# One RWKV chain of 16 matrices in 32-row blocks in place of two chains of 8 in 64-row blocks

## The chip, the cores and the metric

The kernel runs on one core of a Trainium2 chip. The metric is device time in microseconds (us) from the start to the end of one execution.

## The reference, cut to what matters

A decoder trunk of two layers on 256 tokens of 1024 channels, all in fp32. Each layer has a SwiGLU FFN, a token mixer, and a second FFN. The mixer projects the tokens once and runs two branches (RWKV-7 with 8 heads of 64 channels, mLSTM with 4 heads of 128), each merged through a gate of its own:

```python
g_r, g_m = jnp.split(jax.nn.sigmoid(p_g.astype(jnp.float32)), 2, axis=-1)
return ((g_r * y_r + g_m * y_m) @ w_out).astype(h.dtype)
```

The RWKV branch is a recurrence over time, for every head:

```python
sa = jnp.einsum('bhvk,bhk->bhv', s, a_t)
s = s * w_t[:, :, None, :] + sa[..., None] * b_t[:, :, None, :] + v_t[..., None] * k_t[:, :, None, :]
y = jnp.einsum('bhvk,bhk->bhv', s, r_t)
```

The kernel cuts the 256 tokens into 4 chunks of 64. Inside a chunk the recurrence becomes products with 64x64 matrices; one of them is the inverse of (I - N), where N is strictly lower triangular. There are 8 heads x 4 chunks = 32 such matrices a layer.

## The kernel before

Everything is one program with a hand-written order for each engine, and semaphores between them. `mm` (L1792) issues each matmul, `turn` (L1796) each transpose on TensorE; `act` (L680) is every ScalarE operation. An fp32 matmul appears in the trace as two records of weight load and two of matmul, a transpose as one.

In the mixer of a layer TensorE runs, after the projections and the mLSTM products: gate products "num", the turned mLSTM heads, the RWKV chain, the low-rank product "g", gate products "tail", then `branch` m and r and the output product. A gate product is a 128x128 weight tile times 256 tokens, 8 of them accumulate to one tile; 96 of them (6 tiles of 2 x 8 products, `gates`, `GATE_PLACES`) are scattered as lumps over the RWKV chain, so that TensorE has work while VectorE and ScalarE bring one step's result from PSUM to SBUF for the next. There are 24 lumps of 2 to 14.

The chain goes over two groups g of 4 heads (2 pairs q, 2 tiles t of 128 tokens, 2 heads h of a pair), so 8 matrices with the two chunks c of a tile in the lower and upper 64 partitions: 16 matrices of 64x64 a group. In each group:

- "m_t", "m_n": products of a, r with b, k, masked on VectorE (L1625, L1630) into nt (N transposed), mrb, mak, mrk and the three parts n16, o32, o64 of N (blocks of 16; what 32 adds; what 64 adds). Heads and chunks here use all four quadrants of the array.
- v, a, b, k are turned (4 whole 128x128 transposes each).
- The inverse: powers of the 16-blocks p2, p4, p8 and the running product xt, then the steps to 32 and to 64. Each is a `batch` n of 4 matrices x 2 chunks, the chunk c from rows c to columns c of the array: two places. ScalarE copies a power (L680), VectorE adds to xt (`grow`, L1651) and transposes in blocks (`flipped`, L1646).
- "z0" (mak times v), "uz" (xt times a and z0), then "gt", "h", "qt", the local part of y (`y_local`), the chain over chunks (`chain`, L1692) and "y".

The order of the inverse on TensorE, with the gate lumps between:

```python
for n in range(2):
    batch("p4", n, 0, p2t, p2, [AC.at(l, f"p2 {g} {n}"), DV.at(l, f"p2t {g} {n}")])
    batch("xt 2", n, 2, p2, xt, [DV.at(l, f"xt 1 {g}"), DV.at(l, f"m_n {g} 2")])
gates(f"inverse {g} a")
for n in range(2):
    batch("p8", n, 0, p4t, n16, [AC.at(l, f"p4 {g} {n}"), DV.at(l, f"p4t {g} {n}")])
    batch("xt 4", n, 2, n16, xt, [DV.at(l, f"xt 2 {g} {n}")])
```

VectorE computes y_m of the mLSTM branch (L1611) just before "m_t"'s masks. The head statistics (`head_sums`, `head_scaled`) of group 0 lie inside the chain of group 1; those of group 1 come after its y, while TensorE does "g" and "tail"; `y_turned(0)` comes before branch m, `y_turned(1)` after half of it. Weights come through a ring in SBUF, loaded by SP in order; one slot holds RWKV operands of group 1 until "qt 1", and SP waits for that before it loads branch weights into it.

Of the kernel before, what the change touches and what calls it, by code (L numbers as in the profile page):

```python
# [28 lines left out]
ALU = mybir.AluOpType  # L29
# [3 lines left out]
P = 128  # L33
# [97 lines left out]
def pair_uses(label):  # L131
# [6 lines left out]
GATE_PLACES = (("num", 4), ("heads", 4), ("masks 0 a", 8), ("masks 0 b", 4), ("inverse 0 p", 2), ("inverse 0 a", 2), ("inverse 0 b", 2),  # L138
# [112 lines left out]
def trunk(nc, numbers, x_in, c_in, ada_w, ada_b, norm_g, ffn_w_in, ffn_w_out, mix_w_in, rwkv_mu, rwkv_w0,  # L251
          rwkv_w_up, rwkv_a0, rwkv_a_up, rwkv_g_up, rwkv_k_k, rwkv_k_a, rwkv_r_k, rwkv_ln_g, rwkv_ln_b,
          conv_w, conv_b, gate_b, mlstm_ln_g, branch_r, branch_m, w_out, final_g, out):
    with ExitStack() as ctx:  # L254
# [44 lines left out]
        mask_t = sb("mask_t", [P, 4, 64])  # L299
        mask_n = sb("mask_n", [P, 3, 64])  # L300
# [46 lines left out]
        v_tm = carve(2, TT, P)  # L347
        b_tm = carve(2, TT, P)
        k_tm = carve(2, TT, P)
        az = carve(8, P)  # L350
        region = taken[0]
        layer_sets = [[group_set(set_0), group_set(ring[:, 1024 * held:1024 * held + SLOT])] for held in HELD]
# [16 lines left out]
        taken[0] = region  # L369
        m_t = carve(8, 4, 64)  # L370
        m_n = carve(3, 8, 64)
        p2, p2t, p4t, xt = (carve(8, 64) for n in range(4))
        uz = carve(8, P)
        qt = carve(4, P)
        gt_s = carve(4, 64)
        s_s = carve(4, 64)
        h_s = carve(6, 64)
        diag = carve(4, 64)
# [135 lines left out]
        def _(sp):  # L514
# [36 lines left out]
            for l in range(DEPTH):  # L551
# [16 lines left out]
                for n in range(4):  # L568
# [3 lines left out]
                    if use == HELD_TO:  # L572
                        sp.wait_ge(*DV.at(l, "qt 1"))
# [20 lines left out]
        def _(po):  # L594
# [51 lines left out]

            full = y_r[:, 0, 0:P]
            for n, (size, first) in enumerate(((16, 1), (64, 0), (64, 1), (64, 0))):
                fill(full, 1.0)
                keep(full, ALU.is_ge, -first, [[1, P]], -1, 0.0)  # L650
                diagonal_blocks(full, size)
                of_chunks(mask_t[:, n, :])
            for n, size in enumerate((16, 32, 64)):
# [3 lines left out]
                of_chunks(mask_n[:, n, :])  # L657
            for n in (2, 1):
                po.wait_ge(*PO.last(None))
                po.tensor_tensor(mask_n[:, n, :], mask_n[:, n, :], mask_n[:, n - 1, :], ALU.subtract)\  # L660
# [1911 lines left out]
```

## Time and profile before

| | us |
|---|---|
| median of 3 runs (1440.42 to 1440.79) | 1440.57 |
| the profiled execution: its span (the time shown for it) | 1437.0 |
| TensorE matmuls busy | 1419.4 |
| VectorE busy | 1048.7 |
| ScalarE busy | 298.9 |
| from gates "num" to the end of "tail", each layer | 94.67 |

The span runs from the first to the last instruction of one profiled execution; the runs' times are of other executions and hold what lies around it. TensorE is busy in 99% of the span, so a time saved on another engine shows only where TensorE waits for it, and the length of a TensorE record holds its latency: rates are read from differences of starts.

### The profile page before, as it was taken

The page shows a single profiled execution, that of the slowest core. Times are in us where ns is not written, and L with a number is a line of the kernel's source. Part 1 is how long each engine was busy: PE and PEld are TensorE (multiplying, and loading weights), DVE is VectorE, ACT ScalarE, POOL GpSimd, SP SyncE. Part 2 cuts the span into 40 slices and gives each one's busy share as a digit, 9 for nine tenths or more (in the row PEclk, how much of TensorE's full clock was granted, in tenths as well). Part 3 has the DMA queues.
Part 4 walks back from the last instruction along what each step waited for, and adds up shares of the span by engine and source line. Part 5 has one row for each costly group of instructions (what it writes and reads, how often), then busy time and mean ns, then how long its engine had stood idle before and what let it go on. Part 6 is the DMA issues. An engine that isn't in the chain of part 4 may idle for free.

```text
span 1437.0 us, 29272 instructions
## 1 busy us (share of the span) xinstructions
PE 1419.4 (99%) x12848; PEld 1332.5 (93%) x12848; DVE 1048.7 (73%) x1792; ACT 298.9 (21%) x586; POOL 72.2 (5%) x142
## 2 busy tenths in 40 slices
PE   7999999999999999999999999999999999999998
PEld 3999999898988999999999999988898889999998
DVE  5899888787634669987988886787972456756656
ACT  3111102532223031110031110045222311211101
POOL 7100000000000000000000000000000000000000
PEclk9999999999999999999999999999999999999999
DMA  9998876243422657887758876364432247466440
GB/s 348 336 335 302 306 290 195 89 132 104 117 62 90 227 188 260 296 300 292 248 193 266 285 275 235 127 166 132 133 103 61 61 147 263 148 206 205 179 145 30
DMA packets 214046, 283.03 MB, mean 197 GB/s; under 512 B 13288, under 2 KB 177504, under 8 KB 213920
## 3 DMA queue, kind: packets, MB, share of 16 engines
q1 hardware_dynamic: 194976, 211.11, 45.0%
q0 software_dynamic: 17952, 69.21, 13.2%
q8 instruction: 101, 1.65, 0.5%
q10 hardware_dynamic: 992, 0.85, 0.2%
q14 instruction: 25, 0.20, 0.0%
HBM read 280.10 MB, written 1.05 MB: 196 GB/s over the span
## 4 chain that ended last, share of the span: by engine, by line
PE 97%; DMA 1%; SPq 1%; DVE 1%; issue 0%; ACT 0%; ACTq 0%; DVEq 0%
PE ps L1792 96%; DMA arena<-in_ada_w_dram 1%; PE ps L1796 1%; SPq L549 0%; SPq L544 0%; DVE arena L1651 0%; DVE hT L1777 0%; DVE arena L1646 0%; DVE x L1191 0%; ACT xn L680 0%; ACTq L254 0%; SPq L542 0%; SPq L541 0%; DVEq L1776 0%; ACTq L994 0%
## 5 line engine op out<-in xcount | busy, mean ns | idle before, releaser
L1792 PE MATMUL ps<-hT,ring 128*128 128x128 f32 (+2 forms) x2448 | 399.4, 319 | 1.3 <-ACT hT L680 1.3
L1792 PEld LDWEIGHTS ps<-hT,ring 128*128 128x128 f32 (+1 forms) x2448 | 348.1, 190 | 35.5 <-issue 8.6
L1792 PE MATMUL ps<-y_both,arena 128*128 128x128 f32 x2304 | 266.6, 275 | 1.0 <-issue 1.0
L1792 PEld LDWEIGHTS ps<-y_both,arena 128*128 128x128 f32 x2304 | 261.8, 192 | 1.5 <-issue 1.5
L1792 PEld LDWEIGHTS ps<-arena 64*64 64x64 f32 (+1 forms) x3792 | 221.4, 153 | 17.0 <-issue 11.2
L1792 PE MATMUL ps<-arena 64*64 64x64 f32 (+3 forms) x3792 | 235.4, 243 | 1.3
L1792 PE MATMUL ps<-arena,ring 128*128 128x128 f32 (+1 forms) x1312 | 186.5, 294 | 0.0
L1792 PEld LDWEIGHTS ps<-arena,ring 128*128 128x128 f32 x1312 | 171.3, 192 | 6.6
L1018 DVE SCALAR_TENSOR_TENSOR ada_acc<-ada_stage,cond,ada_acc 128x1024 f32<-128x1024 f32 (+1 forms) x119 | 149.0, 1252 | 5.8 <-DMA ada_stage<-in_ada_w_dram 2.2
L1792 PE MATMUL ps<-y_both,ring 128*128 128x128 f32 (+1 forms) x1024 | 150.8, 301 | 0.0
L1792 PEld LDWEIGHTS ps<-y_both,ring 128*128 128x128 f32 x1024 | 138.6, 192 | 6.4
L673 POOL DMA_DIRECT2D ada_stage<-in_ada_w_dram x64 | 45.9, 717 | 1223.5 <-DVE ada_acc L1018 637.6
L1792 PE MATMUL ps<-hT,arena 128*128 128x128 f32 x640 | 78.0, 275 | 0.0
L1792 PEld LDWEIGHTS ps<-hT,arena 128*128 128x128 f32 x640 | 74.7, 192 | 0.0
L1247 DVE TENSOR_TENSOR arena<-ring 128x512 f32<-128x512 f32 x44 | 30.4, 690 | 47.1 <-PE ps L1792 46.8
L680 ACT ACTIVATE xn<-ps 128x128 f32<-128x128 f32 (+2 forms) x18 | 6.9, 383 | 273.7 <-PE ps L1792 273.7
L1121 DVE TENSOR_TENSOR raw<-raw,ps 128x256 f32<-128x256 f32 x40 | 16.8, 420 | 59.1 <-ACT raw L744 58.8
L680 ACT ACTIVATE arena<-ps 128x256 f32<-128x256 f32 (+3 forms) x90 | 39.4, 461 | 80.8 <-PE ps L1792 76.8
L736 ACT ACTIVATE raw<-ps 128x256 f32<-128x256 f32 x40 | 15.4, 386 | 189.9 <-PE ps L1792 189.9
L1232 DVE TENSOR_TENSOR arena<-ring 128x1024 f32<-128x1024 f32 x40 | 48.8, 1219 | 5.5 <-DMA ring<-in_ffn_w_in_dram 5.5
L1238 DVE TENSOR_TENSOR arena<-ring,arena 128x1024 f32<-128x1024 f32 x40 | 49.0, 1225 | 1.4
L1236 DVE TENSOR_TENSOR arena<-arena,ring 128x1024 f32<-128x1024 f32 x40 | 48.7, 1218 | 0.0
(306 smaller groups left out, 1371.8 us busy)
## 6 DMA issues: line engine op xcount, KB each, us to landing
ring<-in_ffn_w_in_dram SPq DMA_DIRECT2D x86, 1024.0 KB, 7.8
ada_stage<-in_ada_w_dram POOLq DMA_DIRECT2D x66, 1024.0 KB, 5.9
ring<-in_ffn_w_out_dram SPq DMA_DIRECT2D x44, 1024.0 KB, 6.2
ring<-in_mix_w_in_dram SPq DMA_DIRECT2D x46, 512.0 KB, 5.0
ring<-in_mix_w_in_dram SPq DMA_DIRECT2D x12, 1024.0 KB, 5.7
ring<-in_mix_w_in_dram SPq DMA_DIRECT2D x6, 1536.0 KB, 6.2
ring<-in_mix_w_out_dram SPq DMA_DIRECT2D x8, 1024.0 KB, 5.2
arena<-in_ada_w_dram SPq DMA_DIRECT2D x6, 1024.0 KB, 13.7
```

The lines of the kernel that those rows point to most:

```text
L673: po.dma_start(wide_stage(v), unit_rows(layer, col, h)).then_inc(ada_full[v % 2], 16)
L680: nc.scalar.activation(out_, in_, func, **kw).then_inc(*AC.step(label))
L736: nc.scalar.activation(part[:, 0, :], ps[:, bank_x, 0:256], ACT.Copy).then_inc(x_copied, 1)
L1018: V.scalar_tensor_tensor(dst, stage[:, k, :], cond[:, k0 + k:k0 + k + 1], dst, ALU.mult, ALU.add).then_inc(ada_done, 1)
L1121: free(V.tensor_tensor(part[:, 0, :], part[:, 0, :], ps[:, bank_w, 0:256], ALU.add))
L1232: V.tensor_tensor(s1, a21, a22, ALU.add).then_inc(w_summed, 1)
L1236: V.tensor_tensor(s2, s1, a11, ALU.subtract).then_inc(w_summed, 1)
L1238: V.tensor_tensor(s4, a12, s2, ALU.subtract).then_inc(w_summed, 1)
L1247: V.tensor_tensor(s1, a21, a22, ALU.add).then_inc(w_summed, 1)
L1792: return nc.tensor.matmul(out_, lhsT, rhs, start=start, stop=stop, **kw)
L1796: return nc.tensor.transpose(out_, in_, ident[0:n, 0:n])
```

## The change

The two groups become one chain: a step takes 16 head-and-tile pairs, 32 matrices, instead of 8 and 16. Every chunk stays in its own half of the partitions (`home`).

- N is made once by 64 products "n" with 32 columns of weights (`quarter`): diagonal 32-blocks and the off-diagonal block. nt is no longer a product: VectorE transposes n16. "mrb" and "kr 0/1" (mak and mrk side by side in mk) are made later, between steps of the chain.
- The inverse works on 32x32 blocks, four of them on the diagonal of the array (`blocks`). `power` multiplies the transposed power pt with px, which holds the power and the running inverse side by side: one product of 64 columns gives the next power and the product to add. Steps: "p2", "px 4", "px 8", "x 8" (inverse of the 16-blocks), "g32", "x 32" (of the 32-blocks), "g64", "xo" (the off-diagonal 32-block), all put together in xf. PO clears its zero block.
- v, b, k are turned by halves of the rows (16 transposes of 64 rows each), a whole (8).
- "uz" to "y" as before, for all 16; ScalarE and VectorE share the copies of uz.
- One lump of gate products a stage: 14 lumps of 4 to 27.
- The statistics of all heads come after the last y; both `y_turned` come after half of branch m. SP waits for "qt".

The diff, cut:

```diff
-GATE_PLACES = (("num", 4), ("heads", 4), ("masks 0 a", 8), ("masks 0 b", 4), ("inverse 0 p", 2), ("inverse 0 a", 2), ("inverse 0 b", 2),
-               ("inverse 0 c", 2), ("uz 0", 2), ("y 0 a", 5), ("y 0 b", 4), ("y 0 c", 2), ("next", 3),
-               ("masks 1 a", 8), ("masks 1 b", 4), ("inverse 1 p", 2), ("inverse 1 a", 5), ("inverse 1 b", 2),
-               ("inverse 1 c", 4), ("uz 1", 2), ("y 1 a", 5), ("y 1 b", 4), ("y 1 c", 2), ("tail", 14))
+GATE_PLACES = (("num", 5), ("n", 6), ("a", 6), ("b", 6), ("c", 5), ("d", 6), ("e", 5), ("f", 6), ("g", 5), ("h", 5),
+               ("i", 4), ("j", 5), ("k", 5), ("tail", 27))
...
+        mrb = carve(16, 64)
+        o64 = carve(16, 32)
+        mk = carve(16, P)
+        xf = carve(16, 64)
...
+        px = carve(2, 16, 32)
+        pt, xt, o32 = (carve(16, 32) for n in range(3))
...
-                        sp.wait_ge(*DV.at(l, "qt 1"))
+                        sp.wait_ge(*DV.at(l, "qt"))
...
+                        po.wait_ge(*PE.at(l, "num"))
+                        po.memset(xf[32:64, :, 0:32], 0.0).then_inc(*PO.step())
+                        po.memset(xf[96:128, :, 0:32], 0.0).then_inc(*PO.step(f"xf {l}"))
...
+                def power(label):
+                    ac.wait_ge(*PE.at(l, label))
+                    for g in range(2):
+                        if g:
+                            ac.wait_ge(*DV.at(l, f"{label} 1"))
+                        act(px[:, 0, 8 * g:8 * g + 8], view(ps[:, 2 + g, :], 8, 64)[:, :, 0:32], ACT.Copy, f"{label} {g}")
...
+                def grow(label, tile):
+                    dv.wait_ge(*PE.at(l, label))
+                    free(V.tensor_tensor(flat(tile), flat(tile), ps[:, 2, :], ALU.add), label)
+
+                def power(label):
+                    dv.wait_ge(*PE.at(l, label))
+                    for g in (1, 0):
+                        part = px[:, 1, 8 * g:8 * g + 8]
+                        if not g:
+                            dv.wait_ge(*AC.at(l, f"{label} 0"))
+                        free(V.tensor_tensor(part, part, view(ps[:, 2 + g, :], 8, 64)[:, :, 32:64], ALU.add), f"{label} {g}")
+                    flipped(None, pt[:, 0:8], px[:, 0, 0:8])
+                    dv.wait_ge(*AC.at(l, f"{label} 1"))
+                    flipped(f"{label} turned", pt[:, 8:16], px[:, 0, 8:16])
...
+                dv.wait_ge(*PE.at(l, "n"))
+                masked(px[:, 0], "n16", 0)
+                dv.wait_ge(*DV.last(l))
+                flipped("nt16", pt, px[:, 0])
+                free(V.tensor_tensor(px[:, 1], px[:, 0], spread[:, :].unsqueeze(1).broadcast_to([P, 16, 32]), ALU.add),
+                     "x 1")
+                masked(o32, "o32", 1)
+                dv.wait_ge(*AC.at(l, "p2"))
+                flipped("p2t", pt, px[:, 0])
+                dv.wait_ge(*PE.at(l, "mrb"))
+                for h in range(2):
+                    free(V.tensor_tensor(mrb[:, h::2, :], view(ps[:, 4 + h, :], 8, 64),
+                                         mask_t[:, 0, :].unsqueeze(1).broadcast_to([P, 8, 64]), ALU.mult),
+                         "mrb" if h else None)
+                power("px 4")
+                power("px 8")
+                masked_mk(0)
+                grow("x 8", px[:, 1])
+                dv.wait_ge(*DV.last(l))
+                flipped("x16", xt, px[:, 1])
+                masked_mk(1)
+                grow("x 32", xt)
+                dv.wait_ge(*DV.last(l))
+                flipped("x64", pt, xt)
+                for r in range(4):
+                    rows, at = slice(32 * r, 32 * r + 32), 32 * (r % 2)
+                    free(V.tensor_copy(xf[rows, :, at:at + 32], xt[rows, :, :]))
+                dv.wait_ge(*PE.at(l, "xo"))
+                free(V.tensor_copy(xf[64:96, :, 32:64], view(ps[64:96, 2, :], 16, 32)), "xf")
...
-                    for n in range(2):
-                        dv.wait_ge(*AC.at(l, f"p2 {g} {n}"))
-                        flipped("p2t", n, p2t, p2)
-                    for n in range(2):
-                        dv.wait_ge(*AC.at(l, f"p4 {g} {n}"))
-                        flipped("p4t", n, p4t, m_n[:, 0])
-                        grow("xt 2", n)
-                    if g:
-                        head_sums(l, y_heads[0], 8, 64, head_sq, "r 0")
-                    for n in range(2):
-                        grow("xt 4", n)
-                    for size, label in ((32, "xt 8"), (64, "xt 32")):
-                        for n in range(2):
-                            grow(label, n)
-                            dv.wait_ge(*DV.last(l))
-                            flipped(f"x{size}", n, p2t, xt)
-                    for n in range(2):
-                        grow("xt 64", n)
...
+                def turned(name):
+                    source = {"v": lambda q, t: raw[:, 8 + q, 1 + t * P:1 + t * P + P],
+                              "b": lambda q, t: sets[q // 2][3][:, 0, q % 2, t * P:t * P + P],
+                              "k": lambda q, t: sets[q // 2][3][:, 1, q % 2, t * P:t * P + P]}[name]
+                    for q in range(4):
+                        for t in range(TT):
+                            at = 64 * (2 * q + t)
+                            for h, hh in enumerate(chunks):
+                                last = nc.tensor.transpose(ps[:, h, at:at + 64], source(q, t)[hh], ident[hh, hh])
+                    last.then_inc(*PE.step(f"turned {name}"))
...
+                def blocks(label, bank, lhsT, rhs):
+
+                    for i in range(16):
+                        for rows in quarter:
+                            last = mm(ps[rows, bank, 32 * i:32 * i + 32], lhsT[rows, i, :], rhs[rows, i, :])
+                    last.then_inc(*PE.step(label))
...
+                def power(label):
+
+                    for i in range(16):
+                        at = 64 * (i % 8)
+                        for rows in quarter:
+                            last = mm(ps[rows, 2 + i // 8, at:at + 64], pt[rows, i, :], px[rows, :, i, :])
+                    last.then_inc(*PE.step(label))
+
+                pe.wait_ge(*DV.at(l, "prep 1"))
+                turned_heads()
+                pe.wait_ge(*DV.at(l, "gates 0"))
+                for q, t, h, hh in heads:
+                    ar, bt, kt, hats = sets[q // 2]
+                    at = 64 * (2 * q + t)
+                    for r, rows in enumerate(quarter):
+                        begin = t * P + 64 * (r // 2)
+                        last = mm(ps[rows, h, at + 32 * (1 - r % 2):at + 64], ar[hh, q % 2, t, 0, rows],
+                                  bt[hh, q % 2, begin:begin + 32 + 32 * (r % 2)])
+                last.then_inc(*PE.step("n"))
+                gates("n")
...
+                pe.wait_ge(*DV.at(l, "nt16"))
+                pe.wait_ge(*DV.at(l, "gates 1"))
+                blocks("p2", 2, pt, px[:, 0])
...
+                last.then_inc(*PE.step("mrb"))
+                gates("a")
+                pe.wait_ge(*DV.at(l, "p2t"))
+                power("px 4")
+                pe.wait_ge(*AC.at(l, "o64"))
+                turned("v")
+                gates("b")
+                pe.wait_ge(*DV.at(l, "px 4 turned"))
+                power("px 8")
+                pe.wait_ge(*DV.at(l, "mrb"))
+                products_mk(0)
+                gates("c")
+                pe.wait_ge(*DV.at(l, "px 8 turned"))
+                blocks("x 8", 2, pt, px[:, 1])
+                pe.wait_ge(*AC.at(l, "turned v"))
+                turned("b")
+                gates("d")
+                pe.wait_ge(*DV.at(l, "x16"))
+                blocks("g32", 3, o32, xt)
+                pe.wait_ge(*DV.at(l, "kr 0"))
+                products_mk(1)
+                gates("e")
+                pe.wait_ge(*AC.at(l, "g32"))
+                blocks("x 32", 2, px[:, 1], px[:, 0])
+                pe.wait_ge(*AC.at(l, "turned b"))
+                turned("k")
+                gates("f")
+                pe.wait_ge(*DV.at(l, "x 32"))
+                for i in range(16):
+                    for c in range(2):
+                        last = mm(ps[quarter[2 * c], 3, 32 * i:32 * i + 32], o64[quarter[2 * c + 1], i, :],
+                                  xt[quarter[2 * c + 1], i, :])
+                last.then_inc(*PE.step("g64"))
...
+                last.then_inc(*PE.step("z0"))
+                pe.wait_ge(*AC.at(l, "turned k"))
...
+                gates("g")
+                pe.wait_ge(*DV.at(l, "x64"))
+                pe.wait_ge(*AC.at(l, "g64"))
+                for i in range(16):
+                    for c in range(2):
+                        last = mm(ps[quarter[2 * c], 2, 32 * i:32 * i + 32], pt[quarter[2 * c], i, :],
+                                  px[quarter[2 * c], 0, i, :])
+                last.then_inc(*PE.step("xo"))
+                gates("h")
+                pe.wait_ge(*PO.at(None, f"xf {l}"))
+                pe.wait_ge(*DV.at(l, "xf"))
+                pe.wait_ge(*AC.at(l, "xo"))
+                pe.wait_ge(*AC.at(l, "turned a"))
...
+                    last.then_inc(*PE.step(f"uz {n}"))
+                gates("i")
+                pe.wait_ge(*AC.at(l, "uz 1"))
+                pe.wait_ge(*DV.at(l, "uz 1"))
...
+                gates("j")
+                pe.wait_ge(*AC.at(l, "h"))
+                pe.wait_ge(*DV.at(l, "gt"))
+                chain_step(1)
+                pe.wait_ge(*DV.at(l, "qt"))
...
+                pe.wait_ge(*DV.at(l, "chain 1"))
+                chain_step(2)
+                gates("k")
+                pe.wait_ge(*DV.at(l, "chain 2"))
...
-                pe.wait_ge(*DV.at(l, "y 1"))
-                y_turned(0)
+                pe.wait_ge(*DV.at(l, "y"))
                 for j in range(4):
                     if j >= 2:
                         pe.wait_ge(*AC.at(l, f"gates {4 + j}"))
                     branch(0, j, y_m, "branch m")
                     if j == 1:
+                        pe.wait_ge(*DV.at(l, "r normed"))
+                        y_turned(0)
```

## Rows read from the trace of the kernel before

In order of time: start us, length us, engine, line, operation, out<-in, partitions*columns of the weights and partitions x moving columns, xcount of records. In windows: length, then busy us (xrecords) of the engine, granted clock, share of DMA, GB/s.

**Rows 1.** The page: engines, granted clock by slice, and the chain that ended last.
```profile
PE 1419.4 (99%) x12848; PEld 1332.5 (93%) x12848; DVE 1048.7 (73%) x1792; ACT 298.9 (21%) x586; POOL 72.2 (5%) x142
...
PEclk9999999999999999999999999999999999999999
...
PE 97%; DMA 1%; SPq 1%; DVE 1%; issue 0%; ACT 0%; ACTq 0%; DVEq 0%
```
**Rows 2.** TensorE from "num" to the end of "tail", layers 0 and 1 (--windows).
```profile
370.02:464.69 94.67, 94.03 (x1602) 1.00 0.28 80
1067.71:1162.38 94.67, 94.04 (x1603) 1.00 0.27 80
```
**Rows 3.** TensorE in order of time, 384 to 403 us: inverse of group 0.
```profile
384.30 1.15 PE L1792 MATMUL ps<-arena 64*64 64x64 f32 x32
385.38 1.13 PE L1792 MATMUL ps<-hT,ring 128*128 128x256 f32 x4
386.44 2.08 PE L1792 MATMUL ps<-arena 64*64 64x64 f32 x64
...
389.51 3.95 PE L1792 MATMUL ps<-arena 64*64 64x64 f32 x128
...
394.45 3.92 PE L1792 MATMUL ps<-arena 64*64 64x64 f32 x96
398.30 1.13 PE L1792 MATMUL ps<-hT,ring 128*128 128x256 f32 x4
399.36 3.17 PE L1792 MATMUL ps<-arena 64*64 64x64 f32 x64
402.46 1.13 PE L1792 MATMUL ps<-hT,ring 128*128 128x256 f32 x4
```
**Rows 4.** The same view, 372 to 382 us: masked products, gates, turns.
```profile
372.71 1.98 PE L1792 MATMUL ps<-arena 64*64 64x128 f32 x64
...
376.55 0.69 PE L1792 MATMUL ps<-arena 64*64 64x64 f32 x32
377.17 3.72 PE L1792 MATMUL ps<-hT,ring 128*128 128x256 f32 x16
...
381.17 1.47 PE L1796 MATMUL ps<-ident,arena 128*128 128x128 f32 x12
```
**Rows 5.** The same view, other widths; last, all records of the narrow products.
```profile
21.97 0.24 PE L1792 MATMUL ps<-ada_red,spread 128*32 128x4 f32 x8
...
272.94 1.13 PE L1792 MATMUL ps<-low_wa,up_wa 32*128 32x256 f32 x8
...
303.04 1.06 PE L1792 MATMUL ps<-arena,ring 128*128 128x128 f32 x8
303.94 2.84 PE L1792 MATMUL ps<-arena,ada_stage 128*128 128x128 f32 x24
...
L1792 PE MATMUL ps<-ada_red,spread x56: 172/195/269, 22.0 to 1416.1; 128*32 128x4 f32 x24, 128*32 128x48 f32 x8, 128*32 128x40 f32 x8, 128*32 128x32 f32 x8
```
**Rows 6.** The chain of waits in 370.02 to 464.69, by line.
```profile
by line: PE ps L1792 91.6%; PE ps L1796 4.6%; DVE arena L1651 2.5%; DVE arena L1646 0.9%; issue 0.6%
```
**Rows 7.** VectorE, then ScalarE, in order of time, 377 to 403 us.
```profile
377.31 0.69 DVE L1630 TENSOR_TENSOR arena<-ps,mask_n 128x512 f32<-128x512 f32 x1 [0.68 <-PE ps L1792]
...
385.44 0.91 DVE L1646 STREAM_TRANSPOSE arena<-arena 128x256 f32<-128x256 f32 x2 [5.64 <-ACT arena L680]
...
390.70 0.42 DVE L1651 TENSOR_TENSOR arena<-arena,ps 128x256 f32<-128x256 f32 x1 [1.44 <-PE ps L1792]
...
387.17 0.38 ACT L680 ACTIVATE arena<-ps 128x256 f32<-128x256 f32 x1 [1.29 <-PE ps L1792]
...
402.57 0.60 ACT L680 ACTIVATE arena<-ps 128x512 f32<-128x512 f32 x1 [0.28 <-PE ps L1792]
```
**Rows 8.** VectorE in the head statistics of the mLSTM branch (--windows).
```profile
359.88:367.04 7.16, 6.61 (x9) 1.00 0.71 191
```
**Rows 9.** DMA issues between 370 and 500 us: count, KB, us to landing.
```profile
ring<-in_branch_w_mlstm_dram SPq DMA_DIRECT2D x2, 1024.0 KB, 6.1
```

More of the change, by code:

```diff
@@ L1701, in _ @@
+                free(V.tensor_copy(y_q[:, :, :, 0], view(ps[:, 4, :], 2, 4, 64)))
+                link(l, V.tensor_copy(y_q[:, :, :, 1], view(ps[:, 5, :], 2, 4, 64)), "y")
+                y_heads = yn_r.rearrange("p a (b c) -> p a b c", b=8)
+                head_sums(l, y_heads, 16, 64, y_squares, "r")
+                head_scaled(l, y_heads, 16, 64, "r")
                 for p in range(4):
@@ new lines, in _ @@
+                turned("k")
+                gates("f")
+                pe.wait_ge(*DV.at(l, "x 32"))
[4 more added lines that the diff above has]
+                last.then_inc(*PE.step("g64"))
+                pe.wait_ge(*DV.at(l, "kr 1"))
+                for q, t, h, hh in heads:
+                    i, at = 4 * q + 2 * t + h, 64 * (2 * q + t)
+                    for c in range(2):
+                        last = mm(ps[chunks[c], 4 + h, at:at + 64], mk[home(c, h), i, 0:64], v_tm[home(c, h), q, t, hh])
@@ new lines, in _, with chunks_of @@
+                gates("i")
+                pe.wait_ge(*AC.at(l, "uz 1"))
+                pe.wait_ge(*DV.at(l, "uz 1"))
+                def chunks_of(t, first, end):
+                    return range(max(2 * t, first), min(2 * t + 2, end))
+                for q, t, h, hh in heads:
+                    for c in chunks_of(t, 1, 3):
+                        last = mm(ps[hh, 1 + c, 64 * q:64 * q + 64], uz[home(c, h), 4 * q + 2 * t + h, 0:64],
+                                  b_tm[home(c, h), q, t, hh])
@@ new lines, in _, with state, y_of @@
+                last.then_inc(*PE.step("h"))
+                for q, t, h, hh in heads:
+                    i, at = 4 * q + 2 * t + h, (2 * q + t) * 64
+                    for c in range(2):
+                        last = mm(ps[hh, 4 + c, at:at + 64], uz[home(c, h), i, 0:64], mrb[home(c, h), i, :])
+                last.then_inc(*PE.step("qt"))
+                def state(q, c):
+                    return h_s[:, 3 * q, :] if c == 1 else s_s[:, 2 * q + c - 2, :]
+                def y_of(q, t, h):
+                    return ps[:, 4 + h, (4 * t + q) * 64:(4 * t + q) * 64 + 64]
@@ new lines, in chain_step @@
+                def chain_step(c):
+                    for q in range(4):
+                        for h in range(2):
+                            hh = slice(64 * h, 64 * h + 64)
+                            at = 256 * (c - 1) + 64 * q
+                            last = mm(ps[hh, 2, at:at + 64], gt_s[hh, 2 * q + c - 1, :], state(q, c)[hh, :])
+                    last.then_inc(*PE.step(f"chain {c}"))
+                gates("j")
+                pe.wait_ge(*AC.at(l, "h"))
+                pe.wait_ge(*DV.at(l, "gt"))
@@ new lines, in _ @@
+                pe.wait_ge(*DV.at(l, "chain 1"))
+                chain_step(2)
+                gates("k")
+                pe.wait_ge(*DV.at(l, "chain 2"))
+                for q, t, h, hh in heads:
+                    for c in chunks_of(t, 1, 4):
+                        cc = chunks[c % 2]
+                        last = mm(y_of(q, t, h)[cc, :], qt[hh, 2 * q + t, cc], state(q, c)[hh, :],
+                                  start=False, stop=True, skip_group_check=True)
+                last.then_inc(*PE.step("y"))
```

440 lines of the change are left out of this document (171 added, 269 removed).

## The prediction

> **What bounds the kernel now.** The page comes first [rows 1]: TensorE's matmuls fill 99% of the span, the chain that ended last is 97% TensorE, and the granted clock stands at full speed (2.4 GHz) in all 40 slices. Only what TensorE streams, and what it waits for, counts. The second view is the stretch that the diff touches, from the gate products "num" to the end of the gate products "tail": 94.67 us in either layer, 94.0 of them busy [rows 2]. The third is TensorE in order of time inside it [rows 3, 4], read by differences of starts. One product of this program is two records. The reader is to see five rates.
>
> - Products of 64 rows, 64 columns of weights and 64 moving columns that use two places of the array at a time: 64 records more cost 3.95 - 2.08 = 1.87 us, so a round of two records takes 58 ns and a product 58 ns [rows 3].
> - The same products in four places (the two halves of the rows times the two halves of the columns): 32 records in 0.69 us against 1.15 us for 32 records in two places [rows 3, 4]. The round still takes 58 ns; a product costs 29.
> - With 128 moving columns a round takes 111 ns (16 records more cost 1.78 us, [rows 5]); 64 records in four places take 1.98 us [rows 4], which is 16 such rounds with the ends. So a round costs about 5 ns plus 0.83 ns a column.
> - A gate product (128x256) costs 2 x 216 = 433 ns: 12 records more take 3.72 - 1.13 = 2.59 us [rows 3, 4].
> - A change between whole and divided array: two gate products from 385.38 to 386.44 are 1.06 us where 0.87 is work, so 0.19 for a lump; 16 products from 384.30 to 385.38 are 1.08 where 0.93 is work, so 0.145 for entering [rows 3].
>
> Waits come last. From 394.45 to 398.30 stand 48 products in two places, 2.80 + 0.145 by rate, but 3.85 passed: 0.91 us of waiting for VectorE; from 399.36 to 402.46 another 0.24 (0.93 + 1.79 + 0.145 is work) [rows 3]. Twice a layer that is 2.3. The chain of waits agrees: L1651 and L1646 hold 3.4% of the stretch [rows 6].
>
> The rates explain the whole stretch. A group (16 matrices) has, in us: "m_t" 1.79, "m_n" 0.47, 16 turns 1.75 (109 ns each, from 12 in 1.47, [rows 4]), eleven batches of 16 products (ten of the inverse and "z0") 10.27, "uz" 1.79, "qt", "gt", "h" 1.63, local y 1.87, chain 0.47, y 0.47: 20.5, two groups 41.0. Add 96 gate products 41.6, 21 entries 3.0, 20 lumps between divided batches 3.9, waits 2.3, the heads turned and "g", equal in both kernels, 2.8: 94.6, against 94.67.
>
> **The change, by parts, for one layer.**
>
> *The inverse.* Gone: 320 products of 64 columns in two places, 18.7 us. New: the chain on blocks of 32 rows in four places on the diagonal. "px 4" and "px 8" are 64 products each of 64 moving columns: 32 rounds of 58 ns, 1.87 each. "p2", "x 8", "g32", "x 32" are 64 products each of 32 columns. No row shows such a round. By the rate above it takes 5 + 27 = 32 ns, so 1.02 each. "g64" and "xo" are 32 products each in two places, also 32 rounds, 1.02 each. Sum 3.73 + 6 x 1.02 = 9.9: saved 8.8. Bounds for the round of 32 columns: 27 ns (no fixed part) and 58 ns (a 32-column product costs what a 64-column one does, the nearest row). I take 32, since eight records with 32 columns of weights and 4 moving ones, four places, end 0.24 us after the first begins, and no record of this kind lasts under 0.172 [rows 5]: the eight began within 0.07 us, two rounds and the entry between them, so neither the starts nor the narrow loads need 58 ns a round.
>
> The page "TensorEngine Tiling (Array Packing)" of the Trainium skill, section Performance Considerations, speaks against this part: each matmul has some 60 cycles of overhead, so a width of 1 lasts as long as 60. If that holds in columns, 32 of them last as long as 60 and the sum is rival A's, 1426; if it holds in cycles, it changes nothing, since a column takes two of them here (0.83 ns at 2.4 GHz). The eight records agree with the second reading; no row shows the width itself.
>
> *The masked products.* "m_t" and "m_n" (4.5 us) become "n" (64 products of 32 columns of weights, 32 or 64 moving; the wide ones set 16 rounds, 0.95; up to 1.87 at 14.6 ns a record, the densest sustained rate, [rows 3]), "mrb" 0.93 and "kr" 1.79: 3.7, saved 0.8. *Turns* of v, b, k: 16 each with half the rows instead of 8 whole. Weights of 128 columns in two row places do run side by side: eight records of 256 columns take 1.13 us [rows 5], where one after another they would take 1.73. So 8 x 111 ns = 0.89 a set, as before; one by one it would be 1.75, 2.6 more in all. *Unchanged by rate:* "z0", "uz", "gt", "h", "qt", local y, chain and y for all 32 matrices (14.3).
>
> Products after: 9.9 + 3.7 + 3.5 + 14.3 = 31.4 against 41.0: saved 9.6.
>
> *Mode changes.* 21 entries and 20 lumps cost 6.9. Now 13 entries and 13 exits to whole products (0.19 each) cost 4.4, and eight times the division changes without a lump between (as "px 4" to "turned v"). No row shows that; bounds 0 and 0.19, I take 0.17, near an entry: 1.4. Saved 1.1.
>
> *Waits.* Every step of the chain now has 4 to 6 gate products (1.9 to 2.8 us), and mostly another batch, between its product and its next use. The narrowest are these. After "px 4": TensorE does turned v (1.0) and six gates (2.8), 3.8 us. In that time pass a copy of 256 columns (0.38) and one addition (0.42), again both, and transposes of 0.45 [rows 7], with hand-overs of 0.1 some 2.2. After "x 8": add 0.69, transpose some 0.75, 0.3 for the end of the matmul, 1.8 against 3.8. After "uz": ScalarE copies 0.60 [rows 7] plus 0.4, against four gates, 1.9. After "n": y_m holds VectorE until about the end of "n", then mask 0.69 and transpose 0.75 follow, 1.8 with hand-overs, against six gates, 2.8. The least slack is 0.9; what a step takes above it shows in full. After "kr 1" and the four 32-row copies VectorE is free before "xo". So I take 0, bound 2.3 as before: saved 2.3.
>
> *The end.* The head statistics of all heads come after the last y: 7.2 us by the same steps of 128x1024 in the mLSTM branch [rows 8], and 1.3 for the copies. Cover: "g" 1.8, the tail of 27 gate products 11.7, branch m 0 and 1 7.1, so 20.6. Without it they would cost 8.5. The turns move but are as many. VectorE then has some 5 us for y_r and 3 for the gates before branch r 0, behind 7.1 of branch m 2 and 3: branch r 0 needs only y_r and the first gate, 5.9. No stall. *DMA:* SP's wait for the branch weights moves from "qt 1" to "qt", 19 us earlier in the stretch, and 23 us of TensorE work (j, k, y, g, tail) stand behind it. The slots for branch m come free with gates 6 and 7, over 14 us before their use, and such a load lands in about 6 [rows 9]. No cost. The POOL memsets follow "num", 45 us ahead of "uz". No cost.
>
> **The sum.** 9.6 + 1.1 + 2.3 = 13.0 us a layer, 26.0 in two. The profiled span 1437.0 falls to 1411.0. The median of the runs, 1440.57, lies 3.6 above that span, which I leave as it is: 1440.57 - 26.0 = 1414.6.
>
> **Rivals.**
> *A, narrow products cost as wide ones* (12%). Six batches 0.85 more each and "n" 0.9: 6.0 a layer, 12 in all: 1426. For it: nothing in the trace sustains a record each 8 ns. Against it: rows 5's eight records.
> *B, the chain stalls* (12%). One batch in flight instead of two halves, so a hand-over that doesn't fit behind its lump shows in full. It gives the waits back or more, 2 to 3 us a layer: 1420. Against it: the slacks above, none below 0.9.
> *C, half-row turns run one by one* (8%): 2.6 a layer: 1420.
> *D, four row groups don't run side by side* (4%), the other sign. If 32-row products in four places ran one after another, the power steps would take 14.9 instead of 3.7 and the other batches about 14 more: 25 a layer more against 13 saved: 1464. It decides from a mean of about 1.5 products at a time. For it: every divided product here uses halves; no row has more than two row groups. Against it: both halves and quadrants run at their full number.
> The forecast itself has 64%; several of A to C at once can eat the gain, which I give 0.02 out of theirs.
>
> **Numbers.** Own range of the forecast: -2 a layer for the lower bounds of the round and the changes, +2 for small waits: 1410 to 1418. A, B, C reach 1426 and its spread; D is left out, and two of A to C at once. Range 1409 to 1428. A difference under 0.2% (2.9 us) is one that a measurement of this kernel can't tell from none. Faster 0.94, within 0.2% 0.02, slower 0.04.
>
> **What would show it.** The stretch from num to tail is 81.7 us in both layers; "px" batches 2.0 us from start to start, 32-column batches 1.15; it holds 160 products (320 records) and 24 turns more; no wait on VectorE or ScalarE in TensorE's chain inside it. Wrong if a 32-column batch takes 2 us (A), if L1792 waits for the transposes (B), if turned v takes 1.8 (C), if px takes over 3 (D).

## The result: 1426.9 us, and the profile of the kernel after

The changed kernel takes 1426.91 us (median of 4 runs, 1426.53 to 1428.1) against 1440.68 for the kernel before beside it: a ratio of 0.991, 95% interval 0.989 to 0.992. It is 13.8 us faster. The forecast was 26.0 faster, 1414.6; the time lies inside the range (1409 to 1428), at its upper edge, and on the side forecast (faster).

The page of the kernel after, in the same parts as [rows 1], and the row of the queue that brings TensorE's instructions:

```profile
span 1425.5 us, 30461 instructions
...
PE 1400.0 (98%) x13536; PEld 1317.5 (92%) x13536; DVE 1027.9 (72%) x1718; ACT 284.1 (20%) x550; POOL 67.7 (5%) x137
...
PEclk9999999999999999999999999999999999999999
...
q8 instruction: 106, 1.74, 0.5%
...
PE 98%; issue 1%; POOL 0%; DVE 0%; ACT 0%; ACTq 0%; POOLq 0%; DVEq 0%
```

Two things are new beside the shorter span: TensorE has more records, and 1% of the chain is "issue", time in which the engine waited for nothing that the profile shows. The q8 row is read so: 1.74 MB in 106 packets is 16 KB a packet, and 13536 matmul records with as many weight-load records, divided by 106, are 255 instructions a packet. The same stretch as in [rows 2], "num" to the end of "tail", in both layers (length, TensorE busy with its records, granted clock, DMA):

```profile
371.83:461.14 89.31, 83.83 (x1946) 0.96 0.29 82
1064.12:1150.94 86.82, 82.81 (x1946) 0.98 0.30 84
```

The stretch was 94.67 in both layers; 81.7 was forecast. It is 5.36 and 7.85 shorter, 13.2 in all. (The profiled span is only 11.5 shorter, since 16 records of 128x256 at the very start took 5.40 us from start to start in this execution, 11.48 to 16.88, where the kernel before took 3.66: up to 15.05 us they came 427 ns apart, the pace of the half clock, then 216, though the clock row of the page shows no change there. The start of the stretch varies between executions, from 370.0 to 373.0 us in the profiles of this study, so the length of the stretch is the finer measure, above all where a kernel was run once.) Against the forecast 7.6 and 5.1 us are missing, and the busy time is short of the length by 5.5 and 4.0. The chain of waits inside the stretch in layer 0 (start, length, what) says where:

```profile
by line: PE ps L1833 89.8%; issue 6.1%; PE ps L2332 2.2%; PE ps L1837 2.1%
...
375.03 4.43 PE ps L1833 x84
379.46 0.67 issue
380.13 1.55 PE ps L1833 x89
381.68 2.45 issue
384.13 8.77 PE ps L1833 x180
...
402.81 0.95 issue
...
412.63 1.41 issue
```

VectorE, which held 3.4% of the stretch in [rows 6], is gone from it, and ScalarE isn't there either, as forecast. In its place stand four stops, 5.48 us together. (Line 1833 is the helper of all products, 2332 the half-row turns, 1837 the whole turns.) TensorE in order of time at the first two, to be read beside [rows 3, 4]:

```profile
376.36 2.86 PE L1833 MATMUL ps<-hT,ring 128*128 128x256 f32 x12
379.15 0.31 PE L1833 MATMUL ps<-arena 32*32 32x32 f32 x13
380.13 1.55 PE L1833 MATMUL ps<-arena 32*32 32x32 f32 x128 [0.67 <-issue]
384.13 0.80 PE L1833 MATMUL ps<-arena 64*64 64x64 f32 x18 [2.45 <-issue]
...
385.82 5.17 PE L1833 MATMUL ps<-hT,ring 128*128 128x256 f32 x12
390.91 1.99 PE L1833 MATMUL ps<-arena 32*32 32x64 f32 x128
392.83 0.71 PE L2332 MATMUL ps<-ident,raw 64*128 64x64 f32 x16
393.47 2.86 PE L1833 MATMUL ps<-hT,ring 128*128 128x256 f32 x12
```

The first stop falls inside "p2", after 13 of its 128 records, where the code waits for nothing. The second falls inside "mrb", after 13 of its 64 records (the row at 380.13 holds 115 records of "p2" and these 13), and there the code waits for nothing either. Between that stop and the next lie 128 records exactly, then (counted in the same view) 511 to the third and 256 to the fourth: one, four and two times 128, with one record missing. Layer 1 has four stops too, each 18 records later in the program (the first after 31 records of "p2") and again 128, 511 and 256 apart: 0.59, 1.83, 0.55 and 1.04 us. 128 records and their 128 weight loads are 256 instructions, one packet of q8. Behind the two stops the lump of 12 gate records takes 5.09 us from start to start, and 2.79 in the other lumps. The rest of "mrb" before it takes 1.69 us, and 0.95 in run 8 below. The granted clock, from windows in the rest of "mrb", in that lump and in the next one:

```profile
384.13:385.82 1.69, 1.69 (x52) 0.50 0.03 10
385.90:390.80 4.90, 4.90 (x12) 0.53 0.00 0
393.60:396.20 2.60, 2.60 (x12) 1.00 0.97 266
```

So the array ran both at about 1.2 GHz in place of 2.4: 2.3 us lost in the lump and 0.7 in "mrb". In layer 1 the clock fell as the lump began, and 1.7 us were lost (4.45 against 2.79). Stops and half clock together are 8.5 and 5.7 us; without them the stretch is 80.8 and 81.15.

### The profile page after: what moved, and what is told of

It reads as the page before. It is cut to its first block, busy times and chain, and to the rows that moved or that the text cites. A ratio compares the mean times of both kernels' runs of the same rounds, so it can differ in the third digit from the quotient of the medians.

```text
span 1425.5 us, 30461 instructions
## 1 busy us (share of the span) xinstructions
PE 1400.0 (98%) x13536; PEld 1317.5 (92%) x13536; DVE 1027.9 (72%) x1718; ACT 284.1 (20%) x550; POOL 67.7 (5%) x137
## 3 DMA queue, kind: packets, MB, share of 16 engines
q8 instruction: 106, 1.74, 0.5%
## 4 chain that ended last, share of the span: by engine, by line
PE 98%; issue 1%; POOL 0%; DVE 0%; ACT 0%; ACTq 0%; POOLq 0%; DVEq 0%
PE ps L1833 97%; PE ps L1837 1%; PE ps L2332 0%; DVE hT L1818 0%; POOL ada_stage L613 0%; ACT xn L696 0%; ACT hT L696 0%; DVE x L1218 0%; POOL spread L609 0%; ACT x L696 0%; ACTq L252 0%; POOL eps L604 0%; POOL ones L604 0%; POOL ident L609 0%; POOL ident L604 0%
## 5 line engine op out<-in xcount | busy, mean ns | idle before, releaser
L1833 PEld LDWEIGHTS ps<-hT,ring 128*128 128x128 f32 (+1 forms) x2448 | 352.7, 192 | 36.5 <-issue 8.6
L1833 PE MATMUL ps<-arena 32*32 32x32 f32 (+6 forms) x4368 | 213.6, 230 | 9.0 <-issue 8.9
L1833 PEld LDWEIGHTS ps<-arena 32*32 32x32 f32 (+3 forms) x4368 | 202.6, 138 | 19.4 <-issue 16.7
L1259 DVE TENSOR_TENSOR arena<-ring 128x1024 f32<-128x1024 f32 x40 | 48.7, 1218 | 0.7 <-DMA ring<-in_ffn_w_in_dram 0.7
L1260 DVE TENSOR_TENSOR arena<-ring 128x1024 f32<-128x1024 f32 x40 | 48.7, 1217 | 0.0
```

Of the source, the lines that this page charges most:

```text
L1259: V.tensor_tensor(s1, a21, a22, ALU.add).then_inc(w_summed, 1)
L1260: V.tensor_tensor(s3, a11, a21, ALU.subtract).then_inc(w_summed, 1)
L1833: return nc.tensor.matmul(out_, lhsT, rhs, start=start, stop=stop, **kw)
```

## The experiments

**Theory I**: TensorE's instructions come in blocks of 256, a next block follows the one before no sooner than some 3.5 us, and batches of short products run through a block faster. **Theory II**: the array itself stops between products of 32 rows. **Theory III**: results of VectorE or ScalarE are late, and the profile names it "issue". All runs beside the kernel before (1440.45 to 1441.15). "Stretch" is num to the end of tail, layer 0 and layer 1; "stops" are the issue waits of 0.2 us and more in it; where "one run" stands the time is that of a single one. Runs 2 and 7 to 10 compute another result than the reference.

| run | time, us | stretch | stops in it |
|---|---|---|---|
| after | 1426.9 | 89.31, 86.82 | 5.48, 4.01 |
| 1: gates moved ahead of the tail | 1423.4 | 87.77, 83.46 | 4.03, 2.86 |
| 2: p2 in wide products (one run) | 1418.7 | 84.96, 81.97 | 3.91, 1.87 |
| 3: 64 tiny products at p2 (one run) | 1433.4 | 91.48, 91.2 | 6.72, 5.63 |
| 4: the same in the tail (one run) | 1427.2 | 88.44, 88.15 | 4.54, 4.35 |
| 5: six gates after p2 | 1418.9 | 83.96, 82.50 | 2.81, 1.97 |
| 6: gates placed by count | 1415.6 | 84.94, 81.09 | 2.72, 0.41 |
| 7: all 32-column batches wide | 1411.5 | 80.63, 80.85 | 0.86, 0.78 |
| 8: after, small gate loads | 1416.5 | 82.81, 84.54 | 2.41, 2.52 |
| 9: by count, small gate loads | 1412.1 | 80.57, 80.80 | 0.36, 0.54 |
| 10: before, small gate loads | 1440.2 | | |

**1. Gate products moved from the tail into the lumps between the batches.**

```
-GATE_PLACES = (("num", 5), ("n", 6), ("a", 6), ("b", 6), ("c", 5), ("d", 6), ("e", 5), ("f", 6), ("g", 5), ("h", 5),
-               ("i", 4), ("j", 5), ("k", 5), ("tail", 27))
+GATE_PLACES = (("num", 5), ("n", 8), ("a", 12), ("b", 7), ("c", 8), ("d", 9), ("e", 9), ("f", 9), ("g", 5), ("h", 5),
+               ("i", 4), ("j", 5), ("k", 4), ("tail", 6))
```

> Gate products of the changed kernel moved from the tail (27 to 6) into the lumps beside the dense batches (n 8, a 12, b 7, c 8, d 9, e 9, f 9); same work. Theory I (TensorE's instructions arrive in blocks of 256 and one block takes 3.5 us or more to follow the last, so batches of many short products run dry): the waits put down to issue in a stretch, 5.5 and 4.0 us, fall below 1 us each, the half clock after them is gone, the stretch from num to tail is about 82 us in both layers, and the time about 1415. Theory II (the array itself stops between 32-row products): nothing changes, 1427. Theory III (a late hand-over from VectorE or ScalarE that the trace names issue): falls as in I, since the lumps hide it too.

Measured: 1423.36 us (1421.65 to 1424.96), 3.6 us faster where theory I wanted 12. The stops behind the lumps that grew are gone; one at "p2" stayed (1.81, in layer 1 1.55), where "p2" and "mrb" follow "n" with only its lump between, and a new one of 2.22 us came at 440.53 in layer 0, in the lump "j"; layer 1 has two small new ones (0.69 and 0.62). The one in "j" has 1403 records from the stop at "p2", 11 times 128 less 5. Places of the blocks fit, sizes not yet; run 8 returns to that.

**2. "p2" with half the instructions**, the same columns streamed (every second block is multiplied by its neighbour's matrix, which gives another result):

```
-for i in range(16):
+for i in range(0, 16, 2):
     for rows in quarter:
-        mm(ps[rows, 2, 32 * i:32 * i + 32], pt[rows, i, :], px[rows, 0, i, :])
+        mm(ps[rows, 2, 32 * i:32 * i + 64], pt[rows, i, :], px[rows, 0, i:i + 2, :])
```

> In the batch p2 one product takes two neighbouring blocks of 32 moving columns with the weights of the first (the second block's result is then not the reference's): 32 products of 64 columns instead of 64 of 32, 128 instructions fewer, the same columns streamed. Theory I: the two waits of 0.67 and 2.45 us around p2 lose at least 1.2 us together and the half clock behind them is shorter or gone, 1.5 to 4 us less in each layer. Theories II (if the stop belongs to 32-row products of any width) and III: no change, within 0.3 us a layer.

**3, 4. The opposite: 64 products of one column more**, 256 instructions that stream almost nothing, ahead of "p2", or in the middle of the tail.

```
+for i in range(16):
+    for rows in quarter:
+        mm(ps[rows, 2, 32 * i:32 * i + 1], ident[rows, rows], ones[rows, 0:1])
```

> 64 products of one column (32x32 weights from the identity, result overwritten by p2) ahead of p2, 256 instructions more. By rate they take 32 rounds of 27 ns, 0.9 us a layer. Theory I: a whole block more must arrive here, 3 to 4 us more in each layer. Theory II: 0.9 plus one more stop at most. Theory III: 0.9.

> The same 64 products of one column in the middle of the gate tail, where each instruction has 108 ns on either side. All theories but II: 0.9 by rate and 0.35 for entering and leaving, 1.2 us more a layer. Theory I says that the stock of one block covers them here and not at p2; theory II says that they cost the same at both places.

Measured: 1418.65 with the half batch, 8.3 us under the kernel after, though only one batch a layer was changed and such a batch streams in 1.2 us. The stretch is 4.35 and 4.85 us shorter, a little over the 1.5 to 4 of theory I. TensorE in order of time at that place, half batch:

```profile
379.55 0.41 PE L1833 MATMUL ps<-arena 32*32 32x64 f32 x13
380.24 1.59 PE L1833 MATMUL ps<-arena 32*32 32x64 f32 x83 [0.28 <-issue]
381.65 0.65 PE L1833 MATMUL ps<-ring 64*64 64x64 f32 x32
382.23 2.86 PE L1833 MATMUL ps<-hT,ring 128*128 128x256 f32 x12
```

The 2.45 us stop is not there, nor the half clock. (Further on, at 403.60, this run has one of 2.60, where the kernel after has 0.95.) The tiny products cost 6.5 us at "p2" (1433.36) and 0.2 in the tail (1427.15), where their 128 records take 1.17 us from start to start and no stop stands beside them (two layers of 1.17 are 2.3 us, but both stretches together are only 0.5 longer, since the stops came out 0.9 shorter in layer 0, and the time before the stretch is 1.8 shorter than in the profile of the kernel after). At "p2" they bring a third stop:

```profile
381.56 1.90 PE L1833 MATMUL ps<-arena 32*32 32x32 f32 x128 [2.21 <-issue]
385.01 0.80 PE L1833 MATMUL ps<-arena 64*64 64x64 f32 x18 [1.56 <-issue]
```

Between the two starts pass 3.45 us for one block. Instructions that stream almost nothing and whose results nobody uses cost what their place makes of them; II and III have no room for that.

**5. Six gate products between "p2" and "mrb"**, taken from the tail; a new place "m" in the programs of TensorE and ScalarE. (Six products are 2.8 us of work, 382.04 to 384.83 below; the 1.4 of the expectation is half of it.)

```
-GATE_PLACES = (("num", 5), ("n", 6), ("a", 6), ...  ("tail", 27))
+GATE_PLACES = (("num", 5), ("n", 6), ("m", 6), ("a", 6), ...  ("tail", 21))
...
 blocks("p2", 2, pt, px[:, 0])
+gates("m")
```

> The kernel after, with six of the tail's 27 gate products moved to one new place, between the second power (p2) and the mrb products; nothing else moves. Theory I (TensorE's instructions come in blocks of 256, and several microseconds after the last block was begun; short products run through them faster than that): the 2.45 us stop between p2 and mrb goes, and with it most of the half clock behind it (about 2.3 us in one layer, 1.7 in the other); other stops may shift by where the blocks now end. Six gates are 1.4 us of work, which covers about that much. I expect 0 to 1 us of idle time there, 2.5 to 4 us less per layer, 1420 to 1422 us. Theory III (a result of VectorE or ScalarE is late before mrb): the same cover would also hide that, but the stop after 13 of p2's own records, which waits for no other engine, would stay, and the half clock with it: 1424 to 1426 us. Theory II (the array stops between products of 32 rows): 1427, unchanged.

Measured: 1418.88 us (1417.76 to 1419.43), 8.0 better than the kernel after with six products in another place, and below the 1420 to 1422 expected. The two stops of 0.67 and 2.45 have become one of 0.31, and the clock stays full (1.00 in both layers):

```profile
380.94 1.17 PE L1833 MATMUL ps<-arena 32*32 32x32 f32 x115 [0.31 <-issue]
382.04 2.86 PE L1833 MATMUL ps<-hT,ring 128*128 128x256 f32 x12
384.83 0.69 PE L1833 MATMUL ps<-arena 64*64 64x64 f32 x32
```

**6. All lumps by the number of instructions ahead of them** (the version that the theory points to, with the whole computation kept).

```
+GATE_PLACES = (("num", 5), ("n", 7), ("m", 6), ("a", 6), ("b", 7), ("c", 7), ("d", 8), ("e", 7), ("f", 8),
+               ("g", 5), ("h", 5), ("i", 5), ("j", 7), ("k", 5), ("tail", 8))
```

> The kernel after, with its 96 gate products placed by the number of instructions of the batch ahead of them: six between p2 and mrb (new place), 7 after n, 6, 7, 7, 8, 7, 8 in the lumps a to f, 5, 5, 5, 7, 5 in g to k, 8 in the tail in place of 27. Theory I: issue waits of at most 1 us a layer in the stretch and no half clock; the stretch 82 to 83.5 us instead of 86.8 to 89.3, the kernel 1415 to 1419 us. If the tail's gates had been hiding work of VectorE (theory III turned round) the time would show as waits on DVE behind the tail and the kernel would not be under 1422. Theory II: 1427.

Measured: 1415.56 us (1414.73 to 1416.61), ratio 0.983 (0.981 to 0.984) to the kernel before: as theory I said, and the fastest kernel of this study that keeps the whole computation. Layer 1 has one stop of 0.41 us. Layer 0 has one of 2.43, more than the 1 us I allowed, with a half clock behind it.

**7. All four 32-column batches wide** ("p2", "x 8", "g32", "x 32").

```
-for i in range(16):
+for i in range(0, 16, 2):
     for rows in quarter:
-        mm(ps[rows, bank, 32 * i:32 * i + 32], lhsT[rows, i, :], rhs[rows, i, :])
+        mm(ps[rows, bank, 32 * i:32 * i + 64], lhsT[rows, i, :], rhs[rows, i:i + 2, :])
```

> The kernel after, with all four batches of 32-column products (p2, x 8, g32, x 32) issued as 32 products of 64 columns each instead of 64 of 32: the same columns go through the array with half the instructions; the second of each pair of blocks is then multiplied by the first one's matrix, which is another result. Theory I: 512 instructions fewer a layer at the four densest places, no half clock, issue waits under 1 us a layer: the stretch near the forecast of 81.7 us (minus up to 0.5 for fewer weight loads), the kernel 1413 to 1417 us. Theory II (the array stops between products of 32 rows, per column): 1425 to 1427. Against the run with p2 alone halved (1418.7) theory I wants 1 to 5 us less.

Measured: 1411.45 us (1410.88 to 1412.65), 1.6 under the lower end of what I expected. The same columns in the same array: what the lost time hung on was the number of instructions, not the columns.

**8, 9. Why some stops are long: small loads of gate weights.** One stop of run 6 came after seven gate products, hardly a dense place. The view of DMA engines, 400 to 420 us in that kernel, in 40 slices of 0.5 us, busy tenths and GB/s:

```profile
DMA  9995000000010000003699999930000001000000
GB/s 316 289 292 127 0 0 0 0 0 0 0 33 0 0 0 0 0 0 39 135 314 348 344 307 289 267 86 0 0 0 0 0 0 33 0 0 0 0 0 0
...
q8 instruction: 4, 0.07, 1.4%
```

A lone 33 is a packet of 16 KB: a block of instructions, at 405.5 and 416.5. In between runs a load of 1 MB from 409.0, and the block that moved with it (found in windows of 0.2 us) did so at 413.2, with the load's last bytes. TensorE stood from 413.47 to 415.90. In the kernel after, the packets at 381.6 (no load) and 411.4 (in a load) are followed by a restart some 2.5 us later. So the two kernels again, with six of eight gate loads a layer cut to one eighth:

```
+ks = slice(0, 1 if ct >= 2 else 8)
-sp.dma_start(view(slot(l, use, 2048), 2, 8, P)[:, n], win[:, :, col + ct * P:col + ct * P + P])
+sp.dma_start(view(slot(l, use, 2048), 2, 8, P)[:, n, ks], win[:, ks, col + ct * P:col + ct * P + P])
```

> The kernel after, with six of the eight loads of gate weights a layer cut from 1 MB to one eighth (one of eight row blocks is loaded, the gate products use what else lies in the buffer); the products and their order are the same. Question: why are the stops of theory I of such different length? In the traces so far a block's packet on the instruction queue moved 0.8 to 1.5 us after the block before it was begun where no weights were loading, and only near the end of a load of gate weights where one was running; the array went on 2.1 to 2.6 us behind the packet. Theory I with the load as a part of the delay (Ia): the two later stops (0.95 and 1.41 us in layer 0, 0.55 and 1.04 in layer 1), whose packets moved in a load, fall to under 0.4 us each; the first two (0.67 and 2.45; 0.59 and 1.83) have no load between them: 2.45 and 1.83 stay within 0.6 us. The kernel 1421 to 1425 us. Rival (Ib): the delay is that of the instruction queue alone, whatever else is loading: all stops as before, 1426 to 1428 us.

> The same cut of the gate weights' loads in the kernel with the gate products placed by count. Theory Ia: its one large stop, 2.43 us in layer 0 at a block whose packet moved at the end of a 1 MB load, goes to under 0.4 us and the half clock behind it too: 1411.5 to 1414 us (as the run with halved 32-column batches, 1411.5). Rival Ib: the stop stays near 2.4 us, 1415 to 1416 us.

Measured: 1416.46 us (1413.96 to 1417.8) for the kernel after, 10.4 less, more than Ia wanted: the stop at the first block had a load before it too (its packet moved at 377.6, at the end of one), which my expectation overlooked, and that place now has one stop of 1.40 (layer 1: 1.63) where there were two. The last one of each layer (1.41 and 1.04) is gone. The one inside "x 8" of layer 0 is still 1.01 (0.95 before the cut), against my expectation: the view of the DMA engines has no load near its packet in either kernel (in this run none from 388 to 398 us), so the dense batches are enough for it. The rest of "mrb", at full clock here, from 380.50 to 381.45:

```profile
380.50 0.50 PE L1834 MATMUL ps<-arena 64*64 64x64 f32 x18 [1.40 <-issue]
...
381.45 2.86 PE L1834 MATMUL ps<-hT,ring 128*128 128x256 f32 x12
```

The kernel by count takes 1412.05 (1410.49 to 1412.31). Its large stop, at the same instruction, seven gates into lump "f" (first row the kernel by count, second the same with small loads):

```profile
415.90 3.74 PE L1833 MATMUL ps<-hT,ring 128*128 128x256 f32 x9 [2.43 <-issue]
```

```profile
412.65 2.10 PE L1834 MATMUL ps<-hT,ring 128*128 128x256 f32 x9 [0.36 <-issue]
```

Nine records take 3.67 us from start to start in the one (the clock halves again) and 2.04 in the other. The same view of the DMA engines, small loads: the packet moves at 410.2, not 413.2.

```profile
GB/s 0 0 0 0 0 0 0 0 0 33 0 0 0 0 0 4 131 125 2 0 33 0 0 0 0 0 0 33 0 0 0 0 0 0 0 33 0 0 0 0
```

The new stop of run 1 is of this sort: its packet moved at 440.2, in the load of a branch's weights, 10.2 us after the packet before.

**10. Control: the same small loads in the kernel before.**

> A control: the kernel before the change with the same cut of six of its eight loads of gate weights a layer to one eighth. The cut took 10.4 us from the kernel after. If it does so through the blocks of instructions alone (theory Ia), it does nothing here, since the kernel before shows no issue wait in this stretch (94.03 of 94.67 us busy): 1439 to 1442 us. If the smaller loads help in another way (the buffers' weights arrive earlier, less traffic beside everything), it takes several us here too: under 1436 us.

Measured: 1440.21 us (10 runs) against 1440.56, ratio 0.9996 (0.9986 to 1.0005). The loads cost nothing where blocks of instructions aren't run through so fast: their cost in the changed kernel goes through the blocks.

## Why the prediction came out as it did

The sum by rates was right, the **Waits** term was not. Its three parts, for a layer:

- *Products*, saved 9.6. Right in sum, a little low. "px 4" takes 1.92 us from start to start (390.91 to 392.83; forecast 2.0), a 32-column batch 1.22 (forecast 1.15): the 32 ns a round stand, 27 and 58 were the bounds. But the rule behind them, 5 ns a round and 0.83 a column, does not hold down there, and that it gave the right figure is luck: by it 32 rounds of one column are 0.2 us, and run 4 took 1.17, hardly less than 32 columns take. "n" takes 1.40 (1.1 was forecast, 1.87 the bound). The half-row turns were put too high: 16 take 0.64 us where 0.89 and a change of 0.17 stood, so 1.2 a layer better for three sets. The 111 ns were a round of 128 moving columns, and a half-row turn moves 64, as its row says. With nearly no stops (run 9) the stretch is 80.57 and 80.80 against 81.7.
- *Mode changes*, saved 1.1. Not measured by themselves. Run 9 without its stops is 1.5 and 1.4 under the forecast in its two layers; the turns explain 1.2 of it, "n" and the 32-column batches take 0.5 the other way and "px" gives 0.2, so some 0.5 us is left, which may lie here or in the products taken as unchanged.
- *Waits*, "So I take 0". This is the step that failed. For the waits that it listed it was right: none of VectorE or ScalarE is in the chain. But the new program has dense places: "p2" is 128 matmul records and 128 weight loads in 1.2 us, 9.5 ns a matmul record, and "mrb" half as many in 1.1 (run 5), where the kernel before took 1.87 us for 64 records [rows 3], 29 ns each. At that rate a block, 128 such records, lasts 3.7 us; now it lasts less than the 3.45 us that the next one needs to come, and TensorE stood 5.5 and 4.0 us. I asked only whether the array can start a record each 8 ns, not whether its instructions arrive so fast. The half clock behind the stop, 3.0 and 1.7 us, was no term at all.

The Trainium skill speaks of this: "Runtime: NRT & Kernel Launch", section Instruction fetch mechanics, says that instructions are refilled in blocks of 256 (16 KiB) over a DMA queue of the sequencer's own while the current one runs, and that the crossing is mostly hidden. The first half the trace agrees with: 255 a packet, and stops whole multiples of 128 records apart. The second half does not hold here: up to 2.45 us a block, 9.5 us a kernel. By that rule the forecast would have stood at 1414.6; the measured time is 12.3 above it.

Rivals. *A* (narrow products cost as wide): refuted by 1.22 us; that its 1426 is the measured time is chance. *B* (the chain stalls, 1420): a stall did take the gain, but not its own: the hand-overs are hidden, and its signature, a wait on VectorE, is absent. *C*: refuted, 0.64 us for 16 turns. *D*: refuted, 1.92 for "px 4". *The end*: right, no stop between "tail" and the branches in any view. In run 6 the tail keeps 8 of its 27 products and no wait on VectorE shows behind it, so even that cover was wider than needed.

What was read rightly or wrongly in the signatures: the stretch "81.7 in both layers" was the wrong statement, and its difference between layers (89.3 and 86.8) is itself a mark of blocks: the same code, with the blocks' ends 18 records apart. The 344 records more (1946 against 1602) and the absent waits on VectorE and ScalarE were as stated.

Open: what makes the clock halve. It fell at or behind stops of 2.45, 2.43, 2.22, 1.83, 1.81 and 1.63 us, but not behind those of 1.55 (run 1) and 1.40 (run 8), nor behind one of 2.60 (run 2). And what a block waits for from the start of its packet to the restart, 2.2 to 2.7 us, no view shows; the packet itself is about 1.1 us of it (0.5% of 16 engines' span for 106 packets). Nor was another order of loads tried, that leaves gaps for the blocks with the whole computation kept.

## What to carry to other kernels

When an edit makes products shorter, count instructions per microsecond beside columns: where two neighbouring batches issue over 256 of them (matmuls and weight loads) in under 3.5 us, put long work between them, and give each lump a size by the instructions ahead of it, not by the latency that it has to cover. An "issue" wait in the middle of a batch, a multiple of 128 records from the last one, is a block of instructions that came late; look then in the DMA view for a load that it came in. The same six products were worth nothing in the tail and 8 us in the right gap.

## What the runs showed of the hardware beyond that

- A block of TensorE's instructions followed the one before it by no less than 3.45 us (381.56 to 385.01, run 3) with no load running; the kernel after has 3.47 (1072.47 to 1075.94) and run 4 has 3.45 again. It comes in two parts: in run 3 the packet moved at 382.6, 1.0 us after the block before was begun, and TensorE went on 2.4 us behind it. A packet held by a 1 MB load makes it longer; cutting those loads was worth 10.4 us in a kernel that TensorE bounds to 98%, and nothing in the one before.
- Products of one column, four row groups: 64 of them (128 records) in 1.17 us, hardly less than 32 columns take (1.22). Here the records, not the columns, set the time, so a 32-column batch is already about as short as this form gets.
- Half-row turns in pairs (64 rows, 128 columns of weights, two places): 16 in 0.64 us, 40 ns each, where a whole turn took 109 ns in the kernel before [rows 4].
